# Most gate tiles of a gated token mixer computed in pairs by seven block products in a stage of their own

## The reference

```python
proj = jnp.einsum('bsnk,nkd->bsnd', branches, w_branch)             # branches: 4 x 512 wide
gates = jax.nn.sigmoid(x @ w_gate + b_gate).reshape(b, L, N_BRANCH, D_MODEL)
merged = jnp.sum(gates * proj, axis=2)
return merged @ w_out
```

## Time and profile before

| | us |
|---|---|
| median of 3 runs | 2140.64 (2140.28 to 2140.71) |
| profiled execution, span | 2136.8 |
| TensorE busy, 10482 matmuls | 2093.7 (98%) |
| VectorE busy | 1488.6 (70%) |
| ScalarE busy | 934.5 (44%) |
| GpSimd busy | 804.2 (38%) |

### The profile page before, as it was taken

One profiled execution on the slowest core, in us unless ns is written; L12 is line 12 of the kernel. 1 busy time (PEld: TensorE's weight loads), 2 busy tenths in 40 slices (PEclk: granted clock), 3 DMA queues, 4 the chain that ended last, 5 costly groups with the idle time before them and its releaser, 6 DMA issues.

```text
span 2136.8 us, 28634 instructions
## 1 busy us (share of the span) xinstructions
PE 2093.7 (98%) x10482; PEld 1749.6 (82%) x10482; DVE 1488.6 (70%) x2541; ACT 934.5 (44%) x1674; POOL 804.2 (38%) x630
## 2 busy tenths in 40 slices
PE   9999999999999999999999999999999999999998
PEld 7788888788888888888888888878788888888886
DVE  4976767867788666667667664277877777776668
ACT  4565563126631255664126564232433334334540
POOL 2133332223322233332223332334666565655651
PEclk9999999999999999999999999999999999999999
DMA  4201101120012311112120001241566665558862
GB/s 135 35 21 30 30 16 35 45 55 21 16 45 79 89 40 31 40 45 74 45 55 21 21 16 50 74 158 50 156 189 202 184 195 171 157 198 305 269 217 93
DMA packets 198621, 198.05 MB, mean 93 GB/s; under 512 B 25161, under 2 KB 157257, under 8 KB 198481
## 3 DMA queue, kind: packets, MB, share of 16 engines
q1 hardware_dynamic: 196000, 187.79, 28.9%
q10 hardware_dynamic: 2480, 8.43, 1.1%
HBM read 151.06 MB, written 45.12 MB: 92 GB/s over the span
## 4 chain that ended last, share of the span: by engine, by line
PE 81%; DVE 12%; issue 3%; ACT 3%; POOL 1%; DMA 1%; DVEq 0%; ACTq 0%; POOLq 0%
PE pair L785 23%; PE pair L1171 13%; PE pair L801 13%; PE obank L1171 5%; PE obank L911 4%; PE chunk L890 4%; PE pair L1200 4%; PE pair L1130 3%; DVE o_top L1993 3%; PE pair L862 3%; PE pair L863 2%; PE chunk L1200 2%; PE obank L1200 2%; DVE act_lo L2247 1%; DVE pt_lo L2173 1%
## 5 line engine op out<-in xcount | busy, mean ns | idle before, releaser
L1845 POOL TENSOR_TENSOR w_lo<-w_raw,w_hi 128x1024 fp32r<-128x1024 f32 (+1 forms) x102 | 217.9, 2137 | 521.7 <-ACT w_hi L1409 521.4
L785 PE MATMUL pair<-act_hi,w_hi 128*128 128x512 f32 x656 | 259.7, 396 | 4.0 <-DVE act_lo L2247 2.0
L785 PE MATMUL pair<-act_lo,w_hi 128*128 128x512 f32 x656 | 255.6, 390 | 0.0
L785 PE MATMUL pair<-act_hi,w_lo 128*128 128x512 f32 x656 | 253.7, 390 | 0.0
L1409 ACT ACTIVATE w_hi<-w_raw 128x1024 fp32r<-128x1024 f32 (+1 forms) x102 | 94.0, 921 | 329.0 <-PE pair L785 323.3
L2173 DVE TENSOR_TENSOR pt_lo<-chunk,pt_hi 128x512 fp32r<-128x512 f32 (+1 forms) x272 | 173.6, 639 | 85.6 <-ACT pt_hi L1437 81.9
L1437 ACT ACTIVATE pt_hi<-chunk 128x512 fp32r<-128x512 f32 (+1 forms) x272 | 150.6, 554 | 174.7 <-PE chunk L890 173.4
L1893 POOL TENSOR_SCALAR prob<-prob,att 128x256 f32<-128x256 f32 (+4 forms) x172 | 117.4, 692 | 243.6 <-DVE att L2109 243.6
L801 PE MATMUL pair<-act_hi,w_hi 128*128 128x512 f32 x432 | 187.3, 434 | 1.1 <-DVE heads L2114 0.9
L1993 DVE TENSOR_SCALAR_CACHE_REDUCE o_top<-score,stat 128x384 uint8<-128x384 f32 (+1 forms) x186 | 164.9, 943 | 14.1 <-issue 13.0
L801 PE MATMUL pair<-act_hi,w_lo 128*128 128x512 f32 x432 | 170.9, 396 | 0.0
(11 more groups left out here) (363 smaller groups left out, 5157.8 us busy)
## 6 DMA issues: line engine op xcount, KB each, us to landing
down_sums<-dn_sums SPq DMA_DIRECT2D x40, 512.0 KB, 6.4
w_raw<-in_w_in SPq DMA_DIRECT2D x37, 512.0 KB, 3.8
w_raw<-in_w_gate SPq DMA_DIRECT2D x32, 512.0 KB, 4.0
up_raw<-in_w_up SPq DMA_DIRECT2D x22, 512.0 KB, 4.8
gate_raw<-in_w_ffn_gate SPq DMA_DIRECT2D x22, 512.0 KB, 6.0
hidden<-gelu_s SPq DMA_DIRECT2D x22, 512.0 KB, 3.4
dn_raw<-down_sums SPq DMA_DIRECT2D x44, 256.0 KB, 4.0
h_in<-down_sums SPq DMA_DIRECT2D x44, 256.0 KB, 4.7
```

What stands on the lines that cost most here:

```text
L785: last = nc.tensor.matmul(dst[0:cols, s:s + HALF], w[:, k, :], a[:, k, s:s + HALF], start=(i == 0), stop=(i == len(order) - 1))
L1845: nc.gpsimd.tensor_tensor(split_into(1, g), w_raw[:, g % 2, 0:kt * cols], split_into(0, g).bitcast(F32), ALU.subtract).then_inc(lo_ready, 1)
```

## The change

22 of the 32 gate tiles are computed ahead of all branches, in a step `gates` that follows `scores`. Two tiles form a 2 x 2 block of weights and x a 2 x 2 block of (four row blocks) x (512 tokens); seven block products of 12 matmuls in place of eight give the four results. It needs sums of x's blocks (made once: GpSimd adds, ScalarE rounds, VectorE takes the low part), per pair four sums of weight blocks and seven splits on GpSimd, seven roundings on ScalarE, and five combinations on VectorE. The gates after sigmoid go to DRAM (`gates_dram`) and are loaded again in the merge. Three gate tiles of B (`FILLER_GATES`) replace B's q, k and v beside the scores; four tiles, gate 0 of each branch, stay beside the attention, and three stay early gates of C. B's q, k and v follow the gates, with nothing beside them. A merge has only its branch tiles; the first two are opened half by half. In A and D GpSimd adds prob to mid. C's merge also splits the merged sum for the output projection. The parts of top-k and of the window counts are distributed anew.

```diff
-MERGE_PARTS = {B: (4, 13, 5, 4), A: (4, 12, 4, 3), D: (4, 8, 3, 0), C: (0, 0, 0, 0)}
+TOPK_GATES = {1: 2, 6: 2, 2: 2, 5: 1, 7: 2, 3: 1, 4: 2}
+TOPK_MERGE = {B: (2, 4), A: (2, 1), D: (2, 4), C: (0, 0)}
+TOPK_FIRST = {("k", A): 7, ("q", A): 6}
...
-SCORE_PARTS = (5, 2, 1, 1, 2, 1, 2, 2, 2, 2, 1, 2, 2, 2, 2, 2, 3, 2, 3, 1, 2, 1, 2, 0, 3)
-Q_UNIT, K_UNIT = 8, 15
+SCORE_PARTS = (5, 1, 1, 1, 1, 1, 1, 1, 1, 1, 2, 1, 2, 1, 2, 1, 2, 1, 1, 1, 1, 1, 1, 1, 0)
+XS_UNITS = {10: 0, 14: 1, 20: 2, 23: 3}
...
+FILLER_GATES = [(B, 1), (B, 2), (B, 3)]
+STORED_GATES = {B: range(1, NKT), A: range(1, NKT), D: range(1, NKT), C: range(1, NKT - len(EARLY_GATES))}
+GATE_TILES = [(br, dt) for br in BRANCH_ORDER for dt in STORED_GATES[br] if (br, dt) not in FILLER_GATES]
+NGATE = len(GATE_TILES) // 2
...
-    out = [("x",), ("ik_f_iw",), ("iq", 0), ("iq", 1), ("iw",), ("scores",)]
+    out = [("x",), ("ik_f_iw",), ("iq", 0), ("iq", 1), ("iw",), ("scores",), ("gates",)]
...
+            def early_fillers():
+
+                pe.wait_ge(pair_free[1], tiles[1].n)
+                for at, banks in enumerate(([pair[1][:, half_cols(s)] for s in range(2)], obank, chunk)):
+                    if banks is chunk:
+                        pe.wait_ge(chunk_free, chunks.n)
+                    yield from project_banks(banks, filler_full)
+                    tile_released.append((filler_full, 2 * at + 2))
...
+                elif kind == "gates":
+                    pe.wait_ge(filler_taken, 1)
+                    pe.wait_ge(relu_done, IDX_HEADS * NSC)
+                    for q, (n, p) in enumerate(GATE_PRODUCTS):
+                        if p == 1 and n >= 2:
+                            pe.wait_ge(gate_second_taken, n - 1)
+                        elif p == 2:
+                            pe.wait_ge(gate_first_taken, n + 1)
+                        elif p == 6 and n >= 2:
+                            pe.wait_ge(gate_combined, 5 * (n - 2) + COMBINED[4])
+                        elif p == 5 and n >= 2:
+                            pe.wait_ge(gate_combined, 5 * (n - 2) + COMBINED[3])
+                        elif p == 5:
+                            pe.wait_ge(filler_taken, 2)
+                        elif p in (7, 3, 4):
+                            pe.wait_ge(gate_combined, 5 * n + COMBINED[{7: 6, 3: 5, 4: 7}[p]])
...
                 elif kind == "merge":
...
-                            project(gate_tile(dt), act_hi, act_lo)
...
+                    opened = []
+                    for ks in ((0, 1), (2, 3)):
+                        for dt in range(2):
+                            if ks[0] == 0:
+                                opened.append((*weights(O_TILES, P), next_pair(dt)))
+                                branch_used[br, dt] = (dt, tiles[dt].n)
+                            hi, lo, dst = opened[dt]
+                            for s in (0, HALF):
+                                for k in ks:
+                                    if dt == 0 and s == 0:
+                                        pe.wait_ge(split_done, splits.next())
+                                    for n, (w, a) in enumerate(((hi, o_hi), (hi, o_low(br)), (lo, o_hi))):
+                                        last = nc.tensor.matmul(dst[:, s:s + HALF], w[:, k, :], a[:, k, s:s + HALF],
+                                                                start=(k == 0 and n == 0),
+                                                                stop=(k == O_TILES - 1 and n == 2))
+                            if ks[-1] == O_TILES - 1:
...
+            def load_gate_tile(br, dt):
+
+                if dt >= 2 and br == B:
+                    tile, use = branch_used[br, dt - 2]
+                    sp.wait_ge(pair_free[tile], use)
+                elif dt >= 2:
+                    sp.wait_ge(sum_done, sums_of(br) + dt - 1)
+                if (br, dt) in FILLER_GATES:
+                    sp.wait_ge(filler_stored[FILLER_GATES.index((br, dt))], 16)
+                else:
+                    at = GATE_TILES.index((br, dt))
+                    sp.wait_ge(gate_stored[at % 2], 16 * (at // 2 + 1))
+                sp.dma_start(prob[:, dt % 2, :], gates_dram[br, dt]).then_inc(gate_in[dt % 2], 16)
...
+                        sp.wait_ge(obank_full, 16 * (BRANCH_ORDER.index(step[1]) + 1))
+                        load_gate_tile(step[1], 1)
+                    if ring.n in gates_before:
+                        load_gate_tile(*gates_before[ring.n])
+                    if ring.n in (ring_at["q", B, 0], ring_at["k", B, 0]):
+                        sp.wait_ge(gate_op_lo, GATE_AT[NGATE - 1, 4] + 1)
...
+                    for k in range(2):
+                        load_gate_raw(1, k)
+                    for n in range(NGATE):
+                        if n + 2 < NGATE:
+                            sp.wait_ge(gate_op_lo, GATE_AT[n, 4] + 1)
+                            for k in range(2):
+                                load_gate_raw(n + 2, k)
+                        for k in range(2):
+                            sp.wait_ge(gate_made[k], n + 1)
+                            br, dt = GATE_TILES[2 * n + k]
+                            sp.dma_start(gates_dram[br, dt], gate_out[k]).then_inc(gate_stored[k], 16)
                 if step == ("attn", B, 0):
...
+            def take_filler(i, src, buf):
+
+                act.wait_ge(filler_full, 2 * i + 2)
+                if i == 0:
+                    act.wait_ge(late_params, 16)
+                elif i == 1:
+                    act.wait_ge(filler_stored[0], 16)
+                nc.scalar.activation(buf, src[:, :], ACT.Sigmoid, bias=gate_bias_of(*FILLER_GATES[i])).then_inc(filler_taken, 1)
+                act.wait_ge(filler_taken, i + 1)
+                act.dma_start(gates_dram[FILLER_GATES[i]], buf).then_inc(filler_stored[i], 16)
...
+                for first in (0, 2):
...
+                        return x_block(p, part, k).bitcast(F32)
+
+                    for k in ks:
+                        told(x_sum_raw(5, k), part_of(21, 0, k), part_of(11, 0, k), ALU.subtract)
+                    for k in ks:
+                        told(x_sum_step(k), part_of(21, 1, k), part_of(11, 1, k), ALU.subtract)
+                    yield
+                    for k in ks:
+                        after_both()
+                        told(x_sum_raw(5, k), x_sum_raw(5, k), x_sum_step(k), ALU.add)
...
+            def gate_weight_sums(n):
+
+                pool.wait_ge(gate_raw_loaded[n % 2], 32 * (n // 2 + 1))
+                if n == 0:
+                    pool.wait_ge(relu_done, IDX_HEADS * NSC)
+                else:
+                    pool.wait_ge(gate_op_lo, max(GATE_AT[n - 1, p] for p in SUM_OF) + 1)
+                (a1, a2), (b1, b2) = ([tile[:, half_cols(s)] for s in range(2)] for tile in gate_raw_of(n))
+                s5, s6, s7, s3 = (gate_sums[:, k, :] for k in range(4))
+                pool_minus(s5, b1, b2, ALU.add)
+                pool.wait_ge(gate_sums_made, 4 * n + 1)
+                pool_minus(s6, s5, a1)
+                pool_minus(s7, a1, b1)
+                pool.wait_ge(gate_sums_made, 4 * n + 2)
+                pool_minus(s3, a2, s6)
...
+            sums_of_x = x_sums()
...
-                if step[0] == "attn":
+                if step[0] in ("x", "ik_f_iw", "iq", "iw", "scores"):
+                    if step[0] == "x":
+                        split_weights(2)
+                        pool.wait_ge(params_loaded, 32)
+                        nc.gpsimd.tensor_scalar(sink_neg[:], sink[:], -1.0, None, ALU.mult).then_inc(consts_ready, 1)
+                        pool.wait_ge(x_taken, 2 * NTOK)
+                    elif step[0] != "iw":
+                        split_weights()
+                    for _part in range({"x": 2, "ik_f_iw": 2, "iq": 1, "iw": 2, "scores": 0}[step[0]]):
+                        next(sums_of_x, None)
+                elif step[0] == "gates":
+                    for q, (n, p) in enumerate(GATE_PRODUCTS):
+                        if (n, p) in ((0, 1), (1, 6)) or (n >= 2 and p == 1):
+                            gate_weight_sums(n)
+                        gate_operand_lo(q)
+                elif step[0] == "merge" and step[1] != FINAL:
+                    for dt in range(NKT):
+                        split_weights(ring_at[step] + dt + 4 - ring.n)
+                        if step[1] in (A, D):
+                            tile, use = branch_used[step[1], dt]
+                            pool.wait_ge(pair_free[tile], use)
+                            if step[1] == D and dt in SPILLED:
+                                pool.wait_ge(mid_loaded[dt], 16)
+                            nc.gpsimd.tensor_tensor(mid[:, dt, :], mid[:, dt, :], prob[:, dt % 2, :], ALU.add
+                                                    ).then_inc(sum_done, 1)
...
+                elif kind == "gates":
...
+                        if p != 1 and p != 2:
+                            dve.wait_ge(gate_product, q + 1)
```

(24 more changed lines are left out.)

512 lines of the change are left out of this document (320 added, 192 removed).

## The result

The changed kernel takes **2229.01 us** (median of 4 runs, 2225.31 to 2243.26); the kernel before took 2140.68 in the same comparison (2140.28 to 2144.18). The ratio is 1.0424, with a 95% interval of 1.0392 to 1.0456: slower by 4%, on the side that the prediction gave 0.82, but 17 us above the upper end of its range and 48 above its value. The profiled execution, of span 2227.2, is of the shorter kind.

What follows compares the result with a forecast made beforehand. TensorE, busy 2093.7 of 2136.8 us, was taken to bound the kernel. Waits opened by removing gate tiles sum to 70.5, less 29.9 gained: +40.6 on 2140.6, so 2181 us, range 2133 to 2212; slower given 0.82.

Steps and rivals of the forecast that it cites:

- The gain: Gates stage: seven block products instead of eight save 2.73 us a pair, 11 pairs, -29.9 us (132 matmuls), called sure.
- Prologue: Ahead of the scores: GpSimd's 18 sums over x delay weight splits and TensorE's first filler; +6 us, bounds 3.8 and 10.
- the end of the gates stage: B's first weight load queues behind the last two stores, so load, rounding and split stand bare: +10 us (9 to 12).
- D: D's merge: uncovered entry and end, growing distance sets, VectorE clashing with GpSimd's adds (+13): +21 us (7 to 29).
- the stretches of A and B: Merges of A and B: bare waits at entry and end, +7 us each (B 5 to 10, A 6.7 to 12).
- The scores' idle: Scores stage: bare filler parts and VectorE's low parts in the relu, multiply-add and release cycle; +8 us, bounds +1.4 and +15.
- the gates stage: GpSimd's and VectorE's work fits each 19.04 us pair with little over; operand and relu waits, taken +5 us.
- The third rival: GpSimd or VectorE bounds the gates stage: 22 us there, 10 in the prologue, total 2202; above 2199 given 10%.
- C's merge: Bare entry and end waits, 7.7 less 0.8: +6.5 us (5.5 to 9); today's wait ahead of the output projection goes.
- The entries: Start of each merge: TensorE waits for VectorE's memset behind gate 0's sigmoid; 5.5, 5.3, 5.5 and 6.3 us bare.
- second rival: Faster than before: release comes within the half tile's 2.72 us, so all 22.6 us of entry waits go; 2133, faster 13%.
- The first rival: Milder: GpSimd's clashes fall on slack and the scores recover VectorE's removed counts; 21 us less, 2160; 18%.

Runs made afterwards that it cites:

- the run with fewer parts: Changed kernel with ten top-k parts per pair in the gates stage instead of twelve, three of 31 search bits left out: 2220.52 us, ratio 1.0372.
- the kernel with filled gaps: Changed kernel with superfluous TensorE matmuls, results never read, issued where TensorE waits: 2237.45 us, ratio 1.0453.
- everything together: Changed kernel with spread x sums, B's early loads, ten gates-stage parts (all 31 bits), D's additions on VectorE, three D parts per tile: 2200.53 us, ratio 1.0273.
- fills: Changed kernel with x's sums spread, plus superfluous matmuls in TensorE's gaps: 2220.26 us, against 2218.84 without them.

## Why the prediction was wrong, and where it was right

- **The gain** was right: 132 matmuls are gone, 29.9 predicted, 30.1 by the pace of before.
- **The step that failed** is TensorE's busy time, given as "about 2064". It is 2098.5. The sum priced each gap at its own length and had no term for what TensorE does behind a gap. That term is 34.8 us of the 49.8 that were missed, and with it in the sum, 40.6 would have been 75. About 25 of it are matmuls at the low clock behind the gaps, about 10 what each further stop costs at full clock. The windows of the earlier trace rows all have a clock of 1.00, since nothing pauses there; but the trace of before had its warning in the window from 540 to 545 us, a clock of 0.50 behind three short waits, and the prediction did not look at the clock behind a wait.
- **The waits** sum to 85.7 against 70.5. Prologue, the end of the gates stage, D, and the stretches of A and B came within 2.1 us in idle time each: 8.0 for 6, 11.7 for 10, 23.1 for 21, 5.3 for 7, 7.7 for 7. The scores' idle 7.1 for 8 was right too. Some of this is luck: B's 7.7 is a shorter entry (3.58 for 5.5) and a longer end (5.00 for 1.4). And that the sum with every cost at its high end, 2230, comes so near to 2229 is an accident, since its costs of 119 are all waits and the waits were 85.7.
- **Mis-sized: the gates stage.** "Both fit, with little over" was the error: 15 us of VectorE's work in 19.04 left no room for clashes with GpSimd. VectorE's small instructions of 0.17 us take 1.22 there, and the busy time is 17.5 us a pair (192.76 / 11). Idle 12.0 for 5. The third rival named this stage, but priced it by GpSimd, which took 14.0 us a pair as forecast; the run with fewer parts shows VectorE. The rival's 22 us don't follow from its own figures either: 19.8 for 19.04 over 11 pairs is 8.4, with the 2.5 of the start 11.
- **Mis-sized: C's merge**, idle 10.8 for 6.5. Its entry gap has nearly the size foreseen, 5.72 for 6.3, but another cause: it is ended by the low part of the heads ahead of the first branch tile, not by the memset behind half of it. Two later gaps of 1.50 and 2.23 were not foreseen, and one of 1.54 ahead of the output projection stayed, where the prediction said that today's wait would go.
- **D** was right in size but only half in cause. VectorE instructions of 2 to 3 us beside GpSimd's additions appear as described, and without them the distances are 15.1 us shorter, yet the merge only 2.9. The load of VectorE as a whole bounds it, and the largest gap, 13.69, stands behind the merge and not in it.
- **The entries** (second rival) are partly covered: 3.58 and 3.60 in B and A, under the 5 to 6 forecast, and 2.02 in D.
- **The first rival**, milder, and the second, faster, came nowhere near: nothing recovered what VectorE's removed counts had taken.

## What to carry to other kernels

Before work that covers waits is removed from TensorE, count the gaps that open, not only their length: here each pause of 7 us or more cost its own time and 2.4 to 3.1 us of slow matmuls behind it, and even a short stop at full clock some 0.28. An engine that fits its stage "with little over" may not fit: VectorE's 15 us a pair became 17.5 beside a busy GpSimd. And moving a helper's work to another engine or stage mostly moved the gap: 2.9 us for the additions, 6.4 for D's parts where a wait of 13.69 had vanished, 8 to 11 in the gates stage, of which A's stretch took 8.0 back. Mending a queue's order did pay (5.9).

## What was not expected of the hardware

**VectorE shut out for a whole row of GpSimd instructions.** Executions of the changed kernel come in two lengths, near 2227 and 14 us more, and the profiles of three experiments are of the longer kind. One instruction makes the difference. VectorE's and GpSimd's timeline in the kernel with filled gaps:

```profile
65.54 19.82 DVE L2773 TENSOR_SCALAR score<-prob,iw_t 128x384 f32<-128x384 f32 x1 [7.96 <-ACT prob L1857]
...
65.68 2.39 POOL L2060 TENSOR_TENSOR w_lo<-w_raw,w_hi 128x1024 fp32r<-128x1024 f32 x1
...
82.66 2.48 POOL L2152 TENSOR_TENSOR early_gates<-early_gates,act_lo 128x512 f32<-128x512 f32 x2
```

and the same instruction in the profiled execution of the changed kernel:

```profile
67.11 1.25 DVE L2758 TENSOR_SCALAR score<-prob,iw_t 128x384 f32<-128x384 f32 x1 [10.50 <-ACT prob L1842]
```

With filled gaps it takes 19.82 us, and ends at 85.36, with the end of GpSimd's unbroken row of splits and sums at 85.14. In the profiles of the kernels with VectorE's additions and with ten parts it took 17.17 and 17.30. The scores stage is 81.5 us then, and 66.5 otherwise. By the Trainium skill ("SBUF — State Buffer", section "Who interferes with whom") the two engines hold a shared pair of ports exclusively, and the later one is blocked for the other's whole instruction; the rows agree with that, but here the excluded one didn't get its turn between GpSimd's instructions either. That the back-to-back row is the cause is supported by the kernel with spread sums, where GpSimd's later sums wait for a released unit each: its four runs lie within 3.5 us of each other, and that VectorE instruction takes 2.53 us in its profile. The two other kernels with spread sums (everything together, and fills) have no long run among their eight either, while each kernel without them that was run four times has one to four. Why the same program sometimes escapes was not settled.

**A pause costs more by its count than by its length.** Pauses of 7.3 us (58.2 / 8) cost 2.4 us of slow matmuls each, pauses of 11.7 us (46.7 / 4) cost 3.1.
